# Hybrid decoder layer: initial states turned on VectorE, last adds of each state half on VectorE, one sum moved by one tile of w_out

## The reference, cut to what matters

```python
z = rmsnorm(x, attn_norm_g) @ w_in               # q, k, v, u
A_bar = exp(A * dt); B_bar = (A_bar - 1) / A * B
bu = einsum('ntgh,gph->ntgp', u, B_bar)
bu[:, 0] += A_bar * h0                           # h0: zero for the prompt, given for each of the 8 samples
h = associative_scan over t of h[t] = A_bar * h[t-1] + bu[t]
y = real(einsum(h, C)) + D_skip * u
ssm_out = gelu(y) * sigmoid(gelu(y) @ w_glu + b_glu)
mix = concatenate(rmsnorm(attn, attn_out_g), rmsnorm(ssm_out, ssm_out_g))
h = x + mix @ w_out
y = h + relu(rmsnorm(h, mlp_norm_g) @ w_mlp_up) ** 2 @ w_mlp_down
```

## Time and profile before

| | us |
|---|---|
| median of 3 runs | 1187.63 |
| lowest and highest run | 1187.04, 1189.89 |
| the profiled execution, its own time | 1188.19 |
| its span, first to last instruction | 1186.4 |
| mean granted clock of PE | 0.999 of full speed |

### The profile page before, as it was taken

How to read it: one execution, slowest core, us unless ns; L and a number is a source line. 1 busy time by engine, 2 the same in 40 slices (tenths; PEclk the granted TensorE clock), 3 DMA queues, 4 the chain that set the end, 5 groups by cost and what they waited for, 6 DMA issues and landing times.

```text
span 1186.4 us, 20247 instructions
## 1 busy us (share of the span) xinstructions
PE 1174.4 (99%) x8492; PEld 1104.2 (93%) x8492; DVE 746.8 (63%) x745; ACT 425.9 (36%) x515; POOL 151.3 (13%) x92
## 2 busy tenths in 40 slices
PE   9999999999999999999999999999999999999998
PEld 7677576799999999999999999999999999999998
DVE  7888889899777555555455555445565455565454
ACT  6100012885454333333333333333333333333331
POOL 2432422000000000100000110000110000110000
PEclk9999999999999999999999999999999999999999
DMA  7443333434545555455455455555445554445553
GB/s 289 151 134 116 111 120 114 161 127 140 177 143 169 186 168 170 160 162 176 160 168 170 160 163 174 162 170 166 160 142 195 163 173 162 160 145 184 173 173 118
DMA packets 55192, 190.29 MB, mean 160 GB/s; under 512 B 7864, under 2 KB 10168, under 8 KB 54712
## 3 DMA queue, kind: packets, MB, share of 16 engines
q1 hardware_dynamic: 54824, 188.79, 47.9%
q10 hardware_dynamic: 288, 0.30, 0.1%
HBM read 185.82 MB, written 5.28 MB: 161 GB/s over the span
## 4 chain that ended last, share of the span: by engine, by line
PE 92%; DVE 5%; issue 1%; ACT 1%; DMA 0%; SPq 0%; DVEq 0%; ACTq 0%
PE psum L1360 92%; DVE states L745 1%; DVE states L906 1%; DVE out_turn L948 1%; DVE out_turn L745 1%; DVE turn L745 0%; PE psum L1479 0%; DMA w_raw<-in_w 0%; DVE w_lo L736 0%; DVE q_t L745 0%; ACT mov_b L633 0%; DVE sq_a L745 0%; ACT gate L606 0%; DVE carry_p L745 0%; DVE q_t L966 0%
## 5 line engine op out<-in xcount | busy, mean ns | idle before, releaser
L736 DVE TENSOR_TENSOR w_lo<-w_raw,w_hi 128x1024 fp32r<-128x1024 f32 x292 | 407.1, 1406 | 386.6 <-ACT w_hi L450 385.8
L1360 PE MATMUL psum<-mov_b,w_hi 128*128 128x288 f32 x2624 | 522.3, 295 | 0.3 <-ACT gate L606 0.3
L450 ACT ACTIVATE w_hi<-w_raw 128x1024 fp32r<-128x1024 f32 x292 | 306.2, 1057 | 483.8 <-PE psum L1360 483.2
L1360 PEld LDWEIGHTS psum<-mov_b,w_hi 128*128 128x128 f32 x2624 | 419.8, 188 | 1.6 <-issue 0.7
L1360 PE MATMUL psum<-mov_a,w_hi 128*128 128x288 f32 x2048 | 406.6, 295 | 0.0
L1360 PE MATMUL psum<-mov_b,w_lo 128*128 128x288 f32 x1312 | 385.3, 294 | 0.0
L1360 PEld LDWEIGHTS psum<-mov_a,w_hi 128*128 128x128 f32 x2048 | 327.7, 188 | 0.1
L1360 PE MATMUL psum<-mov_a,w_lo 128*128 128x288 f32 x1024 | 300.7, 294 | 0.0
L1360 PEld LDWEIGHTS psum<-mov_b,w_lo 128*128 128x128 f32 x1312 | 247.6, 189 | 0.0
L1360 PEld LDWEIGHTS psum<-mov_a,w_lo 128*128 128x128 f32 x1024 | 193.3, 189 | 0.0
L1360 PE MATMUL psum<-x_g,w_raw 128*128 128x288 f32 x640 | 164.2, 414 | 0.2 <-DMA w_raw<-in_w 0.2
(11 more groups left out here) (181 smaller groups left out, 520.5 us busy)
## 6 DMA issues: line engine op xcount, KB each, us to landing
w_raw<-in_w SPq DMA_DIRECT2D x335, 512.0 KB, 3.3
h_t<-in_x SPq DMA_DIRECT2D x3, 576.0 KB, 8.4
out_y<-h_t SPq DMA_DIRECT2D x3, 576.0 KB
b_w<-in_b SPq DMA_DIRECT2D x1, 1024.0 KB, 6.9
c_w<-in_c SPq DMA_DIRECT2D x1, 1024.0 KB, 7.5
k_cache<-in_kc SPq DMA_DIRECT2D x1, 1024.0 KB, 5.6
v_cache<-in_vc SPq DMA_DIRECT2D x1, 1024.0 KB, 6.3
out_kc<-in_kc SPq DMA_DIRECT2D x1, 992.0 KB
```

The costliest lines, as they stand in the source:

```text
L450: nc.scalar.activation(hi3[:, n % SLOTS, :], raw3[:, n % SLOTS, :], ACT.Copy) \
L736: nc.vector.tensor_tensor(lo3[:, n % SLOTS, :], raw3[:, n % SLOTS, :], hi3[:, n % SLOTS, :].bitcast(F32), ALU.subtract) \
L1360: return nc.tensor.matmul(out, lhs_t, rhs, start=start, stop=stop)
```

## The change

Three edits. First, POOL no longer turns the initial states; DVE does it with the same five operations, after its second `turn_in` of the first half. Second, of the eight additions of each half POOL does seven; the eighth is done by DVE (`add_last`, two operations of 576 columns) after its sixteenth `turn_in`, and the counts waited for fall from 8 and 16 to 7 and 14. Third, PE sums the attention squares after six k-tiles of "a" and not after five.

```diff
                 if jj == 0 and m >= 2:
-                    dve.wait_ge(turn_added, 8 * half + m - 1)
+                    dve.wait_ge(turn_added, 7 * half + m - 1)
...
+            def add_last(half):
+                part_read(dve, UNIT[f"bu{half}"], HALF_PAIRS - 1)
+                cols = slice(HALF_COLS - 2 * CHUNK, HALF_COLS)
+                re, im = st4[:, :, 0, cols], st4[:, :, 1, cols]
+                link(tt(re, re, turn4[1][:, :, 0, :], ALU.subtract))
+                link(tt(im, im, turn4[1][:, :, 1, :], ALU.add))
+
+            def turn_h0():
+                dve.wait_ge(h0_loaded, 16)
+                parts = [h0_prod[:, k * 448:(k + 1) * 448].rearrange("p (r j n) -> p r j n", r=2, n=7)
+                         for k in range(2)]
+                later = h0v[:, :, :, 1:DEC_BATCH]
+                for k in range(2):
+                    angle = tab4[:, T_COS + k, :, DEC_SEQ - 1:CHUNK - 1:DEC_SEQ].unsqueeze(1) \
+                        .to_broadcast([P, 2, PAIRS, DEC_BATCH - 1])
+                    link(tt(parts[k], later, angle, ALU.mult))
+                linked()
+                link(tt(later[:, 0, :, :], parts[0][:, 0, :, :], parts[1][:, 1, :, :], ALU.add))
+                link(tt(later[:, 1, :, :], parts[0][:, 1, :, :], parts[1][:, 0, :, :], ALU.subtract))
+                linked()
+                rho = disc3[:, MAG, :].unsqueeze(1).unsqueeze(3).to_broadcast([P, 2, PAIRS, DEC_BATCH])
+                tt(h0v, h0v, rho, ALU.mult).then_inc(h0_turned, 1)
...
-            for n in range(HALF_PAIRS):
+            for n in range(2):
                 turn_in(0, n)
+            turn_h0()
+            for n in range(2, HALF_PAIRS):
+                turn_in(0, n)
+            add_last(0)
             dve.wait_ge(decay_filled, DEC_SEQ)
             dve.wait_ge(decay_zeroed, 2)
             dve.wait_ge(h0_turned, 1)
-            dve.wait_ge(turn_added, 8)
+            dve.wait_ge(turn_added, 7)
+            linked()
             scan_samples(0)
...
             for n in range(HALF_PAIRS):
                 turn_in(1, n)
-            dve.wait_ge(turn_added, 16)
+            add_last(1)
+            dve.wait_ge(turn_added, 14)
+            linked()
             scan_samples(1)
...
-            pool.wait_ge(h0_loaded, 16)
-            pool.wait_ge(cos_sin_ready, 1)
...
             def add_turned(half):
-                for m in range(HALF_PAIRS // 2):
+                for m in range(HALF_PAIRS // 2 - 1):
...
-            mix("a", 0, range(5))
+            mix("a", 0, range(6))
             sum_over_features(UNIT["rms_a"], ssq, squares_added, 2)
-            mix("a", 0, range(5, QT))
+            mix("a", 0, range(6, QT))
```

More of the change, by code:

```diff
@@ L1274, in _ @@
         def _(pool):
[L1275 to L1282, removed]
             def tt(out, x, y, op):
```

## The result

| | before | after |
|---|---|---|
| median of 8 runs, us | 1187.95 | 1192.60 |
| lowest and highest run | 1187.04, 1191.53 | 1190.75, 1193.50 |
| the profiled execution, its own time | 1188.19 | 1193.50 |
| its span | 1186.4 | 1191.6 |
| mean granted clock | 0.999 | 0.996 |

The kernel became slower by 4.7 us, a ratio of 1.0034 (95% interval 1.0024 to 1.0044). The forecast was 1189.2, in a range up to 1191.6; the result lies above the range. Clock and time go together in the runs of after: three at 0.997 took 1190.75 to 1192.3 us, five at 0.996 took 1192.54 to 1193.50.

The account below looks back on a forecast made before the run. PE, busy 1174.4 of 1186.4 us, was taken to set the end. Later third pair +1.7, clock +0.8, w_out -0.9 gave +1.6 us: 1189.8 on the profiled execution, 1189.2 as median, range 1185.3 to 1191.6.

Parts of the forecast that it names:

- The folds: DVE's folds of x squared at the start: 3.4 us shorter with POOL idle, of which PE gets 1.4.
- rival A: No blocking in the turn: DVE's operations follow so closely that POOL's wait; 1185.7 us, chance 0.22.
- T: Moment DVE starts the third state pair, which shifts the stage; 45.94 us before, forecast 47.6, 1.7 us later.
- The new wait: PE, near 45 us, idle 4 us until DVE has read the third pair, queued behind the turn.
- The last additions: DVE's eighth addition frees 1.6 us per half; waits at g_kv and g_q0 grow to 4.7 and 2.0; worth 0.
- rival D: The freed 1.6 us come off whole in both halves, on top of rival A; 1182.5 us, chance 0.04.
- w_out: Sum of attention squares: one more k-tile ahead covers PE's wait for `mix_out("s", 0)`; -0.9 us.
- E: Rival: at w_out another limit, such as DVE's chain, takes over and 0.9 is not gained; 1190.1 us, chance 0.04.
- C: Rival: folds don't shorten, because ACT's filling of tables slows them and not POOL; 1190.1 us, chance 0.06.
- The strided read: DVE's turn products read angles with a step of four floats; whole turn taken as 2.7 us, 3.3 by the skill page.
- the clock behind the new wait: PE's 4 us wait near 45 us may bring a 1.2 GHz stretch; taken as 0.8 us, between 0 and 1.7.
- Rival B: Clock stays down at 45 to 56 us, both k-tiles behind the wait nearly 4 us; 1191.8 us, chance 0.09.

Follow-up runs that it names:

- first edit alone: Kernel before with only the turn of the initial states moved to DVE behind its second pair; 1193.24 us, ratio 1.0039.
- third edit's trace: Trace of the kernel before with only the sum of attention squares moved behind six tiles; 1187.99 us, ratio 1.0001.
- POOL waiting: Changed kernel with POOL's first addition held back until DVE's five turn operations are done; 1187.99 us, ratio 0.9988 against before.
- the turn behind the pairs: Changed kernel with DVE's turn moved behind the last addition of the first half; 1184.83 us, in the repeat 1184.97 us.
- the turn ahead of `u_t`: Changed kernel with DVE's turn moved in front of the moving out of g_u0; 1186.01 us, ratio 0.9984 against before.
- the last additions alone: Kernel before with only the eighth addition of each half moved to DVE; 1187.72 us, ratio 0.9999.

## Why the prediction was wrong

**Right.** The folds and the reciprocal came within 0.1 us of the steps, and PE's idle time before the first pairs was 0.67 (0.6), at full clock. The blocking was as argued against rival A: the turn took 5.56 us (5.4) and T moved by 2.2 (1.7); of the difference, 0.3 is g_u0 ending 0.3 us later in this execution. The price of blocking was 2.3 us (2.7), that of the turn alone 3.24 (2.7). The new wait was 3.6 (4), in part by luck: T came 0.5 later than worked out, but PE's k-tile in front of the wait ended at 46.08 and not at 44.9, since the second two pairs took PE 1.97 us and not 1.25. The last additions were worth nothing, with waits of 4.5 and 1.8 us (4.7 and 2.0), which rules out rival D; w_out gave 1.0 (0.9), which rules out E. The short folds rule out C.

**The strided read was under-sized.** Two products of 448 columns took 1.86 us alone, 0.93 each, where I had put 0.55 from contiguous rows and 0.15 each for the step. The Trainium skill, "SBUF — State Buffer" (Door 1: The DMA port swizzle), named the penalty for reads that go from one 16-byte line to the next; the row agrees, and the 3.3 us that I had worked out for that case was right. The same page's lock (Who interferes with whom) is borne out by 3.24 against 5.56 us of DVE and by 2.76 against 4.19 of POOL.

**The step that failed is the clock behind the new wait.** For a fall behind PE's new wait I took 0.8 us, "between 0 and 1.7": at most the price of the stretch of before, and half of it because "part of it would lie in the wait". The stretch was twice as long: 6.8 us, from 50.1 to 56.9, against 3.4 us before, from 40.9 to 44.3. In the changed kernel's trace none of it lay in the wait, and it cost 2.9. In the trace of the first edit alone 1.6 us of it did, and it still cost 1.9, above the bound. That the wait brings it is shown by filling the wait: with two tiles in it the stretch is gone, and the stage is 2.8 us shorter at the same T. Rival B had the mechanism and the place, at a price of 3.4 and a chance of 0.09, and with it a forecast of 1191.8. Its point of decision was not met to the letter: one k-tile behind the wait was slow, 4.21, and the other was at 2.21 again, the rest of the loss being in the pairs.

**A second term was missing**, the fall at 272 us, worth 1.6 in the traced execution. No row of before pointed to it.

**And the base was one draw.** The profiled execution of before had a slow stretch at 41 us, which I took as the kernel's own and as certain. By the third edit's trace, with the same wait and no slow stretch, it need not be: its third pair starts at 44.14. Against that, the changed kernel's T is 4 us late and not 2.2. My sum let the change end a slow stretch that some executions of before (38 of 81 runs are at 1.000) never had, and set too little against it for the loss of clock that all 16 executions with this place of the turn showed.

**What stays open**: why 0.4 us came back between the halves; and whether the fall at 272 us has to do with the change. Its counterpart appeared in the profiles of two kernels without the changed kernel's late turn (267.2 to 270.7 us with POOL waiting, 264.4 to 267.8 in the repeat of the turn behind the pairs). In all three it begins within 1 us behind the end of the same matmuls of the sample attention, and in the other eight traces the clock stays up there: chance again, at one place of the program. No run was made that changes only the work ahead of it.

## What to carry to other kernels

Work moved from an idle engine to a busy one is priced by where it lands: here five operations that cost 3.2 us alone cost 5.6 beside POOL's additions, and next to nothing at two other places. Where the engine that sets the end gets a new wait at the start, give it other tiles to do in the meantime, if they don't come from the cover of a later step, or allow for paying twice, once for the wait and once for the clock. Before a term is read from a slow stretch in one profile, the clocks of the other runs tell how often such a stretch occurs.

## What was not expected of the hardware

- **The same idle time, two outcomes.** 1.96 us of PE idle was followed by 0.50 in the profile of before, 2.03 us in that of the third edit alone by 1.00; 1.61 us left the clock up with the turn ahead of `u_t`, and 1.29 us with POOL waiting did not.
- **The fall does not keep one distance from the wait.** It began 1.6 us before PE was at work again in the first edit alone, 0.4 us behind it in the changed kernel and with the last additions alone, 1.3 us behind it in before, and with POOL waiting 2.1 us behind the longest of its waits (1.29 us; one of 0.48 us lay in between).
- **A fall without a wait.** From 272 to 275 us in the changed kernel the clock is 0.50 with PE busy for the whole of it and for the stretch before. What stood before it are the matmuls of 16 columns for the sample attention (two groups of 32 records, 1.11 us each), and they stood before it in both other traces that have this fall. Before had the same order and kept its clock there. Whether these matmuls have to do with it was not tested.
- **Both sides of the lock pay.** When DVE and POOL each have operations ready, they take turns one instruction at a time. In the changed kernel DVE's first product takes 0.97 us and POOL's first addition beside it 2.08; DVE's second product then takes 2.21 and POOL's second addition 2.15. In all DVE's products take 3.09 us and not 1.86, its sums 1.78 and not 0.70, POOL's additions 4.19 and not 2.76.
- **A step of four floats in one input** of a product costs as much as I had granted for steps in an input and the output: 0.93 us for 448 columns, where 512 contiguous ones take about 0.60.
